# Two layers of a diffusion block with a mixture of experts: where the experts' weights are loaded, and in which order the experts run

## The reference, cut to what matters

```
h = h + gate1 * (y @ w_out)                      # the "output stage"
t = modulate(rmsnorm(h, norm2_w), sh2, sc2)
g = top-1 of softmax(t @ w_group)                # 4 groups
e = top-2 of softmax(t @ w_expert) in that group # 4 experts in each group
out[row] = sum over its 2 experts of weight * (silu(t @ w_gate[e]) * (t @ w_up[e])) @ w_down[e]
h = h + gate2 * out
```

## Time and profile before

| | |
|---|---|
| runs | 1779.41 us (1777.31 to 1781.45) |
| the profiled execution | 1780.7 us, span 1778.8 us |
| TensorE busy | 1506.4 us (85% of the span), mean granted clock 0.929 |
| VectorE, ScalarE, GpSimd busy | 806.2, 466.8, 240.7 us |
| DMA moved | 353.92 MB |
| weights of experts | 33 loads of each of three matrices, 1024 KB each |
| layer 0: output stage, route, experts | 724 to 936, 936 to 973, 973 to 1171 us |
| layer 1: output stage, route, experts | 1475 to 1548, 1548 to 1579, 1579 to 1747 us |

### The profile page before, as it was taken

How to read it: one execution, slowest core, us unless ns; L and a number is a source line. 1 busy time by engine, 2 the same in 40 slices (tenths; PEclk the granted TensorE clock), 3 DMA queues, 4 the chain that set the end, 5 groups by cost and what they waited for, 6 DMA issues and landing times. The chain is left out here.

```text
span 1778.8 us, 18329 instructions
## 1 busy us (share of the span) xinstructions
PE 1506.4 (85%) x7011; PEld 787.7 (44%) x7011; DVE 806.2 (45%) x1317; ACT 466.8 (26%) x957; POOL 240.7 (14%) x246
## 2 busy tenths in 40 slices
PE   4999998999997999799991999649969999649942
PEld 2566554444445777445540333224435554413310
DVE  2136655888842667354324111126546763422214
ACT  5122112000106677221110111023226651100002
POOL 0000000000002685322001000021000001010001
PEclk9999998999998999999995999869979999869976
DMA  8444435777783998733119799662040003399964
GB/s 324 142 130 148 148 107 172 270 281 283 278 246 94 304 279 257 281 114 140 36 52 376 273 356 339 261 254 104 12 90 7 1 1 119 137 383 353 394 259 153
DMA packets 164423, 353.92 MB, mean 199 GB/s; under 512 B 17217, under 2 KB 106641, under 8 KB 145521
## 3 DMA queue, kind: packets, MB, share of 16 engines
q1 hardware_dynamic: 143496, 277.78, 45.2%
q0 software_dynamic: 17056, 61.79, 9.1%
q10 hardware_dynamic: 3785, 13.18, 1.9%
HBM read 296.67 MB, written 56.05 MB: 198 GB/s over the span
## 5 line engine op out<-in xcount | busy, mean ns | idle before, releaser
L595 PE MATMUL ie_pu<-aT_even,ie_w_conv 128*128 128x512 f32 (+1 forms) x640 | 207.4, 486 | 0.0
L2129 PE MATMUL ex_ps_gu<-room,ex_xT 128*32 128x512 f32 x1472 | 170.4, 615 | 31.2 <-DMA room<-in_moe_w_up_dram 27.8
L595 PEld LDWEIGHTS ie_pu<-aT_even,ie_w_conv 128*128 128x128 f32 x640 | 121.2, 190 | 84.6 <-issue 76.5
L1647 PE MATMUL po_ps_y<-po_w,po_yT 128*128 128x512 f32 x320 | 139.1, 592 | 2.0 <-DVE po_n L1546 2.0
L641 PE MATMUL ie_pu<-yacc_even,aT_even 128*128 128x512 f32 x288 | 127.4, 603 | 8.4 <-ACTq L745 8.4
L641 PE MATMUL ie_pu<-hacc,aT_even 128*128 128x512 f32 x288 | 125.2, 593 | 0.0
L2129 PEld LDWEIGHTS ex_ps_gu<-room,ex_xT 128*32 128x32 f32 x1472 | 57.3, 114 | 138.8 <-issue 134.3
L2246 DVE TENSOR_TENSOR ex_hid<-ex_hid,ex_ps_gu 128x256 f32<-128x256 f32 x25 | 10.5, 421 | 215.4 <-ACT ex_hid L2200 215.4
L769 DVE SCALAR_TENSOR_TENSOR yacc_even<-ie_pu,pcol,yacc_even 128x255 f32<-128x255 f32 x80 | 47.5, 614 | 107.7 <-ACT yacc_even L722 106.2
L1647 PEld LDWEIGHTS po_ps_y<-po_w,po_yT 128*128 128x128 f32 x320 | 60.0, 190 | 74.0 <-issue 71.7
L641 PEld LDWEIGHTS ie_pu<-yacc_even,aT_even 128*128 128x128 f32 x288 | 55.3, 193 | 78.8 <-issue 78.8
(11 more groups left out here) (466 smaller groups left out, 2308.3 us busy)
## 6 DMA issues: line engine op xcount, KB each, us to landing
room<-in_moe_w_gate_dram SPq DMA_DIRECT2D x33, 1024.0 KB, 11.5
room<-in_moe_w_up_dram SPq DMA_DIRECT2D x33, 1024.0 KB, 13.9
room<-in_moe_w_down_dram SPq DMA_DIRECT2D x33, 1024.0 KB, 8.9
ie_w_conv<-in_ada_w_dram SPq DMA_DIRECT2D x27, 1024.0 KB, 5.3
yacc_even<-in_ada_w_dram SPq DMA_DIRECT2D x13, 1024.0 KB, 5.4
y<-ex_y ACTq DMA_DIRECT2D x25, 512.0 KB, 8.1
room<-ac_rows SPq DMA_DIRECT2D x12, 1024.0 KB, 6.8
ie_w_conv<-in_ev_w_in_dram SPq DMA_DIRECT2D x10, 1024.0 KB, 6.0
```

Of the source, the lines that this page charges most:

```text
L595: last = nc.tensor.matmul(pu[t][:, a:b], w_conv[h][:, k, t * P:(t + 1) * P], aT[:, k, a:b], start=(k == 0), stop=(k == KD - 1))
L1647: last = nc.tensor.matmul(ps_y[:, c * BANK:(c + 1) * BANK], yT[n % 2][:, k, :] if even else kit.oT[:, k, n * P:(n + 1) * P], (w[:, k] if e ...
L2129: last = MM(ps_gu[s][rows, :, :], xT[s][:, k, rows], wgu[q % RING][:, :, k, :], start=(k == 0), stop=(k == KD - 1))
```

## The change

- `room5` becomes one tensor for the whole program. The rows that the recurrent stage and layer 0's output stage use (`yacc`, `hacc`) lie in it, interleaved by tile, so that tile n fills the place of the n-th 2048 columns; `po_w` and the recurrent stage's scratch lie behind them.
- The output stages load the fixed places' weights in pieces (one matrix each): in layer 0 five of six, each when t of a tile is stored, in layer 1 all nine, three per tile, of three fixed places.
- GpSimd's store of t has two semaphores, and waits for the store of two tiles before.
- The plan (`named`) is computed before the limits, with one more VectorE instruction.
- In `phase_route` the sorted place that is second in order is loaded at once when the plan is known; those from the fourth on wait until both first gathers have landed.
- Places run in a mixed order, with another ring of slots; layer 1 has three fixed places, and other strips, still 13 and 10 passes.
- The small loads for the next stage move from `phase_route` to behind the load of the tenth place in order.

```
-PLACES = [Places(NT, 2, [5, 5, 2, 5, 5, 4, 4, 4, 3, 3, 3, 2, 2, 2, 2, 1]), Places(NT - CT, 2, [4, 4, 0, 4, 4, 3, 3, 3, 3, 2, 2, 2, 2, 2, 1, 1])]
+PLACES = [Places(NT, 2, [5, 5, 2, 5, 5, 4, 4, 4, 3, 3, 3, 2, 2, 2, 2, 1], [0, 4, 1, 5, 13, 12, 10, 3, 7, 6, 9, 15, 11, 14, 8, 2], [0, 4, 1, 2, 3]),
+          Places(NT - CT, 3, [4, 4, 4, 0, 4, 4, 3, 3, 3, 2, 2, 2, 2, 1, 1, 1], [0, 11, 1, 9, 2, 10, 12, 7, 15, 6, 5, 8, 4, 13, 14], [0, 2, 1, 3, 4])]
+EARLY = [2 * 3 - 1, 3 * 3]
...
+        self.slot = {q: ring[i % RING] for i, q in enumerate(order)}
+        self.before = {q: order[i - RING] if i >= RING else None for i, q in enumerate(order)}
+        self.whole = ring[len(order) % RING]
...
+def load_early(kit, sp, layer, piece):
+    q, c = piece // 3, piece % 3
+    if c < 2:
+        kit.load_c(sp, q, PLACES[layer].slot[q], c)
+    else:
+        kit.load_d(sp, q, PLACES[layer].slot[q])
...
@@ phase_out, SyncE @@
+            def early_rows(n):
+                sp.wait_ge(t_stored[n % 2], n // 2 * 16 + 16)
+                load_early(kit, sp, layer, n)
...
                 load_h(n)
+                if not even:
+                    for piece in range(3 * (n - 1), 3 * n):
+                        load_early(kit, sp, layer, piece)
+                elif n >= 2:
+                    early_rows(n - 2)
+            if even:
+                early_rows(count - 2)
@@ phase_route, SyncE @@
-            for q in range(places.fixed):
-                kit.load_gu(sp, q, q)
-                kit.load_d(sp, q, q)
-            sp.wait_ge(kit.t_stored, 16 * N)
-            if layer == 0:
-                kit.load_odd_small(sp)
-            else:
-                kit.load_final(sp)
+            for tiles_stored in kit.t_stored:
+                sp.wait_ge(tiles_stored, 16 * (N // 2))
+            for piece in range(EARLY[layer], 3 * places.fixed):
+                load_early(kit, sp, layer, piece)
+            if layer:
+                kit.load_final_row(sp)
             sp.wait_ge(named, 1)
-            for q in range(places.fixed, RING):
-                if places.strips[q]:
+            for i, q in enumerate(places.order[:RING]):
+                if i == 3:
+                    for rows_loaded in kit.x_loaded:
+                        sp.wait_ge(rows_loaded, 16)
+                if q >= places.fixed:
                     e = sp.value_load(kit.plan[0:1, q:q + 1], min_val=0, max_val=NEXP - 1)
-                    kit.load_gu(sp, e, q)
-                    kit.load_d(sp, e, q)
+                    kit.load_gu(sp, e, places.slot[q])
+                    kit.load_d(sp, e, places.slot[q])
@@ phase_route, VectorE, behind the place @@
+            ch(TT(by_place[:, :, :], across(place[:, :]), down(tab[:, R_NUM:R_NUM + NEXP]), ALU.is_equal))
+            ch(TT(by_place[:, :, :], by_place[:, :, :], across(tab[:, R_NUM:R_NUM + NEXP]), ALU.mult))
+            ch(RED(ident[:, :], by_place[:, :, :], AX.X, ALU.add))
+            ch(V.tensor_copy(kit.plan[:, 0:NEXP], ident[:, :]))
+            dve.sem_inc(named, 1)
@@ behind row_hot @@
-            ch(TT(by_place[:, :, :], at_place[:, :, :].rearrange("p e r -> p r e"), across(tab[:, R_NUM:R_NUM + NEXP]), ALU.mult))
-            ch(RED(ident[:, :], by_place[:, :, :], AX.X, ALU.add))
-            V.tensor_copy(kit.plan[:, 0:NEXP], ident[:, :]).then_inc(named, 1)
@@ phase_experts, SyncE @@
-            for q in range(RING, NEXP):
+            for i, q in enumerate(places.order[RING:]):
                 e = sp.value_load(kit.plan[0:1, q:q + 1], min_val=0, max_val=NEXP - 1)
-                o = before(q)
-                if o is not None:
-                    sp.wait_ge(gu_ready, places.last[o] + 1)
-                kit.load_gu(sp, e, q % RING)
-                if o is not None:
-                    sp.wait_ge(d_ready, places.last[o] + 1)
-                kit.load_d(sp, e, q % RING)
-            sp.wait_ge(d_ready, places.last[before(NEXP)] + 1)
+                sp.wait_ge(gu_ready, places.last[places.before[q]] + 1)
+                kit.load_gu(sp, e, slot[q])
+                sp.wait_ge(d_ready, places.last[places.before[q]] + 1)
+                kit.load_d(sp, e, slot[q])
+                if i == 4:
+                    if layer == 0:
+                        kit.load_odd_small(sp)
+                    else:
+                        kit.load_final(sp)
+            sp.wait_ge(d_ready, places.ends[WHOLE] + 1)
```

More of the change, by code:

```diff
@@ L345, in phase_in_even @@
         w_tail, w_conv = kit.w_tail, kit.w_conv
-        under = [tile[:, :, :].rearrange("p t d -> p (t d)") for tile in (kit.yacc, kit.hacc)]
+        under = [kit.rows[:, a * (NT + 1) * D:(a + 1) * (NT + 1) * D] for a in range(2)]
         w_zvo = [flat[:, 0:KD * BANK].rearrange("p (k n) -> p k n", n=BANK) for flat in under]
@@ L352, in phase_in_even @@
         tokens = [tok_all[:, h, :, :] for h in range(2)]
-        stage = [sb(f"stage{s}", [P, BANK]) for s in range(4)]
+        stage = [kit.beside[:, s * BANK:(s + 1) * BANK] for s in range(2)] + [sb(f"stage{s}", [P, BANK]) for s in range(2, 4)]
         r = {n: kit.room[0:NDT, j * TOK:(j + 1) * TOK] for j, n in enumerate(("x", "e", "ac", "f", "b", "ln", "dt", "da", "keepf", "keepb"))}
@@ L830, in begin_recurrent @@
 def begin_recurrent(kit, scope):
-    kit.room = scope.enter_context(kit.nc.sbuf_tensor("room", [P, 20 * TOK], F32))
+    after = kit.room5[:, 2 * (NT + 1) * D:RING * SLOT]
+    kit.room, kit.beside = after[:, 0:20 * TOK], after[:, 20 * TOK:20 * TOK + 2 * BANK]
     at = 0
@@ L1306, in phase_out @@
     PIECE = 2
+    begin_weights(kit, layer)
     with ExitStack() as st:
@@ L1981, with begin_weights @@
 SLOT = 3 * KD * FF
[L1984 to L1994, removed]
-    kit.xg = two("xg", [P, D])
+def begin_weights(kit, layer):
+    A = kit.A
     GU = 2 * KD * FF
@@ L2026, in phase_experts @@
     places = PLACES[layer]
-    NP, FIXED = places.passes, places.fixed
-    WHOLE = NEXP % RING
+    NP = places.passes
+    WHOLE = places.whole
     WB = NP % 2
-    used = [q for q in range(NEXP) if places.strips[q]]
-    times = [len([q for q in used if q % RING == s]) for s in range(RING)]
-    nth = lambda q: len([o for o in used if o <= q and o % RING == q % RING])
-    before = lambda q: max([o for o in used if o < q and o % RING == q % RING], default=None)
+    times, slot, nth = places.times, places.slot, places.nth
     held = [len([c for c in range(NP) if c % 2 == s]) for s in range(2)]
@@ L2075, in _ @@
                 for s in kit.odd_slots:
-                    sp.wait_ge(d_ready, places.last[before(NEXP + (s - WHOLE) % RING)] + 1)
+                    sp.wait_ge(d_ready, places.ends[s] + 1)
                 kit.load_odd(sp)
@@ L2128, in gate_up @@
                         rows = slice(j * LANE, (j + 1) * LANE)
-                        last = MM(ps_gu[s][rows, :, :], xT[s][:, k, rows], wgu[q % RING][:, :, k, :], start=(k == 0), stop=(k == KD - 1))
+                        last = MM(ps_gu[s][rows, :, :], xT[s][:, k, rows], wgu[slot[q]][:, :, k, :], start=(k == 0), stop=(k == KD - 1))
                 last.then_inc(gu_ready, 1)
@@ L3051, in program @@
         kit.wr = kit.keep("wr", [P, KD, 20])
+        kit.room5 = kit.keep("room5", [P, RING * SLOT])
+        kit.slot = [kit.room5[:, s * SLOT:(s + 1) * SLOT] for s in range(RING)]
         def hold(scope, name, shape):
```

54 lines of the change are left out of this document (33 added, 21 removed).

## The result

The changed kernel takes 1770.07 us (median, 1768.28 to 1770.93), the kernel before 1780.11 on the same chip (1777.31 to 1781.45): ratio 0.9944, 95% interval 0.9934 to 0.9955. The gain is 10.0 us, half of the forecast. The profiled execution has a span of 1769.1 us for 1778.8; it is the slowest of the five.

What follows compares the result with a forecast made beforehand. TensorE, 85% busy, was bounded by waits at the route barriers and for late expert weights, 45 us together. Gains 4.1 + 2.2 - 2 + 6 + 9.5 = 19.8 us gave 1760 us from the median, range 1743 to 1774.

Steps and rivals of the forecast that it cites:

- Starts of the experts: Route-stage barriers: gathers find emptier queues and land sooner, so TensorE starts 4.1 us earlier in layer 0, 2.2 in layer 1.
- The sign: Route stage: SyncE's last loads come after the gathers' landing, its DRAIN is last, and `ex_ps_x` starts at about 969.
- Output stage of layer 1: Weight pieces issued beside GpSimd's loads delay the columns `po_vec`, stalling TensorE: 2 us lost.
- The bounds "0, and about 5": Layer 1's output stage: loss between 0 and about 5 us, the latter if all three pieces go first.
- Passes of layer 0: Layer 0's experts: waits of 4.7 and 5.7 us before passes 10 and 11, 13 us lost for 18.9: gain 6.
- Passes of layer 1: Layer 1's experts: waits 1 us at pass 5, 13 at pass 6; 16.5 us lost for 26: gain 9.5.
- The holes did not vanish: Rival for both expert stages: no weight waits left, 11.84 us a pass, 49 us gained, 1730; chance 0.12.
- The gathers did not starve: Rival in the expert passes: gathers land late beside full queues, 4.1 us wait per pass, up to 1805; slower, chance 0.08.
- The holes only move: Rival: SyncE's waits hold weights in the expert stages, columns cost 5 us, little but the starts gained: 1774; chance 0.2.
- The barrier is held by something else: Rival at the route stages: not the gathers hold the barrier, starts stay: 1766; counted within the forecast's 0.6.
- The range: Whole kernel: 1743 to 1774 us, for 8 in 10.
- the likeliest case's own range: Whole kernel, likeliest case at 1760: 1750 to 1769 us, from the bounds of starts and columns.

Runs made afterwards that it cites:

- Experiment 5: Changed kernel with fourth and fifth place in order issued behind the barrier, no wait for gathers in SyncE's queue: 1766.57 us, 3.5 us below the changed kernel.
- Experiment 1: Changed kernel with layer 1's output-stage pieces one tile later (none with the second tile, six with the third, three with the fourth): 1760.25 us, 9.8 us below it.
- experiment 2: Changed kernel with GpSimd's small column loads issued ahead of the rows in both output stages, pieces unmoved: 1764.08 us, 6.0 us below the changed kernel.
- experiment 3: Changed kernel with the next stage's small loads behind the fifteenth place in order, not the tenth: 1762.9 us, 7.2 us below the changed kernel.
- experiment 6: Changed kernel without SyncE's wait for the two gathers, all places issued as soon as known: 1772.65 us, 2.6 us above the changed kernel.
- experiment 4: Changed kernel with pieces one tile later in layer 1's output stage and small loads behind the fifteenth place in both layers: 1759.55 us, ratio 0.9876.
- experiment 8: Changed kernel with pieces later, columns first, two places behind the barrier, and small loads later in layer 1 only: 1752.21 us, 17.9 us below the changed kernel.

## Why the prediction was right or wrong

**Starts of the experts: right.** 4.5 and 2.2 us for 4.1 and 2.2. The sign was the one named: SyncE issues its last two places at 964.11 to 967.5, behind the gathers' landing, its DRAIN is the last, and `ex_ps_x` starts at 967.92. The gathers went out at the same moments as before (956.6 and 958.0), but the route began 0.6 us earlier (`rt_ps_tot` at 940.83 for 941.47), so inside the stage they were 0.6 us later, where I had 0.7. Experiment 5 shows the price of the issues behind the landing, 4.1 and 2.3 us, as reckoned (2.08 us a place and the DRAIN).

**Output stage of layer 1: the step that failed.** Of the 10 us that the forecast had too much 6.8 are in this term and 3.7 in layer 1's passes. I put it: "its last MB takes 5 to 7.5 us instead of 2.5, and the columns land at 1489 to 1491.4: I take 2 us lost". The share was near, the amount it applies to was not. All of GpSimd's 2.1 MB go out within 3.6 us beside 3.15 MB of pieces and 1.05 MB of h, so the whole queue runs at the reduced share, not its last MB. The same view of 1470 to 1480 us, where both queues are never empty, gives the share:

```profile
q1 hardware_dynamic: 372, 2.76, 65.7%
q0 software_dynamic: 366, 1.31, 35.8%
```

The two queues get as many packets each, but SyncE's are of 7.4 KB and GpSimd's of 3.6 KB, so GpSimd's queue moves 1.31 of 4.07 MB, 32%. At 0.13 MB per us its 2.1 MB take as long as everything that SyncE has issued: SyncE's queue is through at about 1482 and GpSimd's last. The columns, at its end, land after 15.8 us, the last piece after 16.0. That is 7.6 us later than before: as late as if all three pieces had gone first (3.15 MB at 0.42, 7.5 us), my outer bound for the landing. The Trainium skill (DMA: Bandwidth & Descriptors, Queues, rings and completion order), each DMA engine taking its queues in turn by packets, agrees with these rows, 366 packets beside 372; what I drew from it ("2 us or less") doesn't follow from it, since turns protect a queue's share and not the transfer that stands at its end.

The second half of the term wasn't there at all. I charged the slower products after each hole among the passes and none after this one, but the 5.85 us wait is followed by 2.65 and 0.28 us of them. The granted clock by stretch (before, then changed; the eighth figure, 1.00 is the full clock):

```profile
1484.00:1490.00 6.00, 6.00 (x15) 2.52 (x14) 2.31 (x4) 0.00 (x0) 0.00 (x0) 1.00 0.20 77
```

```profile
1484.00:1490.00 6.00, 5.55 (x8) 2.40 (x9) 4.62 (x10) 0.20 (x1) 0.00 (x0) 0.50 0.01 2
```

After the wait TensorE is at 0.50, the lower of its two levels, for the stretch up to 1490. So 7.6 us later, less 1.75 us of slack (I had 2.6), plus 2.93 for the clock is 8.8. Experiment 1 takes the whole of it away (9.8 us, the interval of its ratio being about 3 us on either side; 9.0 in that stretch of the profile); experiment 2 shows that it is the order within the queue that turned a small load into the stall. The bounds "0, and about 5" were too narrow by the clock (2.9 us) and by the slack (0.85).

**Passes of layer 0: right in size, not in place.** 5.0 us for 6. I had 4.7 us before pass 10 and 5.7 before pass 11; it is 7.62, 0.98 and 0.45, 1.4 us less in all, and one slow product in place of two. Against that the chunk, which waits for no DMA and runs at the full clock (7.13 us), waits 1.83 us for the copy of its rows where I took 0.8, and pass 0's own product took 9.24 us where it had taken 8.51. So the size came out right partly by luck: a larger hole than forecast, and fewer slow products.

**Passes of layer 1: mechanism right, size off.** 5.8 us for 9.5. The waits are as reckoned: 0.96 and 13.57 us before passes 5 and 6 where I had 1 and 13. What failed is the part from the chunk, whose 3.8 + 3.0 us I took as all gained: the wait for weights is gone, but ScalarE's copy of the chunk's rows keeps TensorE 2.15 us where I took 0.8 from an ordinary pass (1.3), and the product still takes 8.82 us, not 6.9 (1.9). ScalarE's rows say where the 2.15 come from:

```profile
1720.62 0.34 ACTq L2252 DMA_DIRECT2D y<-ex_y  x1
1721.71 0.59 ACT L2237 COPY ex_xT<-ex_ps_x 128x512 f32<-128x512 f32 x1 [12.50 <-issue]
```

The copy is the same as in a pass, 0.59 us, but it starts 1.4 us after `ex_ps_x` has ended, at 1720.27: in ScalarE's order it stands behind the store of the last pass's result, and in a pass ahead of it. In the kernel before the wait for weights hid this. The other 1.9 us are no fault of the working: in experiments 2 and 3 the same product takes 7.13 us, behind waits of the same length.

**Rivals.** The holes did not vanish. The gathers did not starve: no wait in either table names one. "The holes only move" got the time nearly right (1774) for a reason that was half its own: its 5 us for the columns is nearer the measured 8.8 than my 2, but the passes, which it gives almost nothing, gained 10.8. "The barrier is held by something else" is excluded by the DRAIN rows.

The range held the time; the likeliest case's own range, 1750 to 1769, missed it by 1 us. Its ends came from the starts and the columns with the 5 us bound, and had no room for the clock behind the hole; the passes' own error had no part in that range.

## What to carry to other kernels

When a bulk transfer is moved into a stage with idle DMA engines, take every transfer that this stage issues at the same moment, add up both queues' bytes, and date the *last* of the small ones by the sum, not by its own size; then start the bulk one tile later (9.8 us here) or put the small ones first (6.0). Charge a hole with the slower products behind it wherever it stands, and cost a stage's end (the generic chunk) by its own rows and not by those of the passes ahead of it. Loading early was no gain by itself here: the whole change with the old order was 12 us slower than the kernel before; which of its other parts costs that wasn't taken apart.

## What the runs showed of the hardware

- GpSimd's DRAIN at a barrier lasts until its own gathers have landed: 6.9 to 7.2 us with the weight queue nearly empty (experiment 5; in layer 0 the second gather lands at 960.3, the DRAIN ends at 960.4), 9.7 to 13.4 with it full (experiment 6; 968.0 and 968.0). SyncE's takes 0.13 us in each case, with megabytes of its loads outstanding.
- Two queues with work moved equal numbers of packets (366 and 372 in 10 us) and so bytes about one to two, the one with the smaller packets getting the smaller part; 4 KB at the end of it took 15.8 us for 8.2.
- A wait of 5.85 us cost 2.93 us more in the products behind it; one of 7.62 us cost 2.5 (9.58 us for 7.08), and one of 13.57 us 2.1 (9.14). The longer wait wasn't the dearer. The granted clock was 0.50 over the first, 0.73 and 0.77 over the two others.
- Layer 1's chunk product took 7.13 us in experiments 2 and 3 and 8.7 to 8.8 in the changed kernel and experiments 1, 4, 5, 6 and 8, always behind waits of about 1.5 and 2.15 us. In experiment 3 and in the changed kernel alike the granted clock was 1.00 over the 14 us ahead of it; over the product it was 1.00 and 0.81.
